# Diagonal blocks on opposite corners of the array: level 32 of the delta-rule inverse

## What is computed

```python
a_mat = jnp.where(strict, jnp.einsum('bhncd,bhnmd->bhncm', k_beta, k) * decay_mask, 0.0)
eye = jnp.eye(CHUNK, dtype=jnp.float32)
t_mat = lax.linalg.triangular_solve(a_mat + eye, jnp.broadcast_to(eye, a_mat.shape),
                                    left_side=True, lower=True)
...
def step(state, inp):
    w_c, u_c, attn_c, q_c, k_c, e_c = inp
    v_new = u_c - jnp.einsum('bhcd,bhde->bhce', w_c, state)
    o_c = jnp.einsum('bhcd,bhde->bhce', q_c, state) + jnp.einsum('bhcm,bhme->bhce', attn_c, v_new)
    state = state * e_c[..., None, None] + jnp.einsum('bhcd,bhce->bhde', k_c, v_new)
    return state, o_c
```

## Time and profile before

| | |
|---|---|
| median of 3 runs | 2157.25 us (2155.11 to 2157.98) |
| span of the profiled execution | 2150.7 us |
| TensorE busy | 2070.0 us, 96% |
| VectorE, ScalarE, GpSimd busy | 63%, 30%, 11% |
| mean granted TensorE clock | 0.993 |

### The profile page before, as it was taken

How to read it: one execution, slowest core, us unless ns; L and a number is a source line. 1 busy time by engine, 2 the same in 40 slices (tenths; PEclk the granted TensorE clock), 3 DMA queues, 4 the chain that set the end, 5 groups by cost and what they waited for, 6 DMA issues and landing times. The chain is left out here.

```text
span 2150.7 us, 20753 instructions
## 1 busy us (share of the span) xinstructions
PE 2070.0 (96%) x6898; PEld 1060.6 (49%) x6898; DVE 1364.1 (63%) x1918; ACT 642.5 (30%) x1063; POOL 234.5 (11%) x188
## 2 busy tenths in 40 slices
PE   6999999999999999999899899999999999999998
PEld 5444444446555556566555445554444444444443
DVE  4687753265746746647652578529999997534633
ACT  4345431323443434434311521012321111241021
POOL 0000001112212113122100400001000000003200
PEclk8999999999999999999999999999999999999999
DMA  9333389241111111111420316269722222334021
GB/s 342 110 109 100 116 272 236 89 92 35 47 29 37 38 37 37 24 36 43 147 41 1 108 59 120 74 189 250 173 59 75 68 73 69 103 103 137 20 98 59
DMA packets 243824, 207.17 MB, mean 96 GB/s; under 512 B 52204, under 2 KB 202785, under 8 KB 243745
## 3 DMA queue, kind: packets, MB, share of 16 engines
q1 hardware_dynamic: 213393, 157.25, 24.5%
q0 software_dynamic: 13056, 42.99, 8.2%
q10 hardware_dynamic: 17312, 6.10, 1.2%
HBM read 182.55 MB, written 60.33 MB: 113 GB/s over the span
## 5 line engine op out<-in xcount | busy, mean ns | idle before, releaser
L2300 PE MATMUL bank<-hT,ring 128*128 128x512 f32 x576 | 254.2, 592 | 0.0
L2300 PE MATMUL bank<-resid,ring 128*128 128x512 f32 x432 | 191.3, 592 | 0.0
L2300 PEld LDWEIGHTS bank<-hT,ring 128*128 128x128 f32 x576 | 109.5, 190 | 137.7 <-issue 136.7
L1279 PE MATMUL bank<-hT,ring 128*128 128x512 f32 x336 | 157.7, 595 | 1.8 <-ACT silu_z L1515 1.8
L3220 DVE SCALAR_TENSOR_TENSOR yT<-s_arena,yT 128x1024 f32<-128x1024 f32 x120 | 153.8, 1282 | 0.0
L3220 DVE SCALAR_TENSOR_TENSOR s_arena<-s_arena 128x1024 f32<-128x1024 f32 x112 | 143.5, 1282 | 0.0
L2272 PE MATMUL bank<-hT,ring 128*128 128x512 f32 x320 | 139.4, 594 | 0.0
L2300 PEld LDWEIGHTS bank<-resid,ring 128*128 128x128 f32 x432 | 82.1, 190 | 103.3 <-issue 102.3
L1869 DVE SCALAR_TENSOR_TENSOR memory<-memory,col_exp_last,bank 128x128 f32<-128x128 f32 x64 | 22.3, 348 | 153.7 <-PE bank L1459 153.7
L2272 PEld LDWEIGHTS bank<-hT,ring 128*128 128x128 f32 x320 | 60.2, 190 | 73.7 <-issue 73.4
L2345 PE MATMUL bank<-ssm_y,ring 128*128 128x512 f32 x192 | 83.4, 592 | 0.0
(11 more groups left out here) (585 smaller groups left out, 3671.7 us busy)
## 6 DMA issues: line engine op xcount, KB each, us to landing
ada<-in_ada_w SPq DMA_DIRECT2D x8, 2048.0 KB, 8.1
ring<-in_gdn_in_w SPq DMA_DIRECT2D x32, 512.0 KB, 4.1
ring<-in_w_in SPq DMA_DIRECT2D x54, 256.0 KB, 2.9
ab_U_sums<-in_w_in POOLq DMA_DIRECT2D x6, 2048.0 KB, 19.0
resid<-in_x SPq DMA_DIRECT2D x8, 1024.0 KB, 8.9
ring<-in_lru_in_w SPq DMA_DIRECT2D x16, 512.0 KB, 3.9
ring<-ab_U_sums SPq DMA_DIRECT2D x32, 256.0 KB, 3.0
lru_arena<-in_ada_w SPq DMA_DIRECT2D x6, 1024.0 KB, 12.5
```

The costliest lines, as they stand in the source:

```text
L1279: last = nc.tensor.matmul(bank[:, to, :], w[:, k, :], v[:, k, :], start=(first and k == 0), stop=(k == KB - 1), skip_group_check=not only)
L2300: last = nc.tensor.matmul(bank[:, to, :], w[:, k, :], src[:, k, :], start=(start and k == 0), stop=(k == HK - 1), skip_group_check=not alone)
```

## The change

At level 32 each chunk's 128 x 128 x 128 product becomes two 64 x 64 x 64 ones: the upper left block (`top`) and the lower right one (`under`), each on its own 64 rows and 64 columns of the array. The first matmul of each half is an exception: it reads all 128 rows, with 64 columns. This holds for `Y32` and for `YT32`, in all eight heads. Levels 16 and 64 stay as they are. And `fill(int(n == 0), 4)` becomes `fill(1, 4)`: in heads 0 to 6 one filler step now stands between `Y32` and `YT32`. In head 7 four steps stood there already.

```diff
+                    def each_half_blocks(dst, lhs, rhs, name, before):
+
+                        for n, x in enumerate("ab"):
+                            before(x)
+                            for c in range(n * NCH // 2, (n + 1) * NCH // 2):
+                                for rows_ in (top, under):
+                                    ks = slice(0, P) if (c % (NCH // 2), rows_) == (0, top) else rows_
+                                    last = nc.tensor.matmul(dst[rows_, c, rows_], lhs[ks, c, rows_], rhs[ks, c, rows_], start=True, stop=True)
+                            hd_pe.mark(last, name + x)
+
...
-                            x_, xT_ = (inv, invT) if n else (base, baseT)
-
...
-                            each_half(R4, lambda c: part[n % 2][:, c, :], lambda c: x_[:, c, :], f"Y{s}", settled)
+                            if n == 1:
+                                each_half_blocks(R4, part[1], inv, f"Y{s}", settled)
+                            else:
+                                each_half(R4, lambda c: part[0][:, c, :], lambda c: base[:, c, :], f"Y{s}", settled)
...
-                            fill(int(n == 0), 4)
-                            each_half(R4, lambda c: prod[:, c, :], lambda c: xT_[:, c, :], f"YT{s}",
-                                      lambda x: hd_act.wait(pe, f"prod{s}{x}", h))
+                            fill(1, 4)
+                            if n == 1:
+                                each_half_blocks(R4, prod, invT, f"YT{s}", lambda x: hd_act.wait(pe, f"prod{s}{x}", h))
+                            else:
+                                each_half(R4, lambda c: prod[:, c, :], lambda c: baseT[:, c, :], f"YT{s}",
+                                          lambda x: hd_act.wait(pe, f"prod{s}{x}", h))
```

## The result

The changed kernel takes 2167.28 us (median of 5 runs) against 2157.72 us before; the ratio is 1.005, 95% interval 1.0036 to 1.0065. That is slower by 7.8 to 14 us. The forecast was 2165.2 us, in a range of 2156 to 2178.5.

A forecast was written before the change was run, and what follows sets the result against it. TensorE was taken as the bound almost everywhere, VectorE at the head's end. Sixteen products at 1.93 us plus 6.02 for the filler less 28.97 removed gave +7.9 us, so 2165.2 us, range 2156 to 2178.5.

The forecast's parts named there:

- What bounds the place: Around Y32 and YT32 TensorE works without a gap; at the head's end the order of VectorE's work sets the time.
- The filler, +6.0 us: One 0.86 us step moved from the head's end to between Y32 and YT32, paid in full in seven heads.
- The work added: Each level 32 product has 32 records where it had 16, taking 1.93 us against 1.78 today.
- x: Time of one new level 32 product, first start to what follows: 1.93 us; a gain only under 1.43.
- The way in: Change of form on entering a level 32 product: 0.10 us.
- The three inner switches: Changes between 128-row and 64-row records inside a level 32 product: 0.19 us each.
- The way out: Change of form from a level 32 product to the filler behind it: 0.19 us.
- The pairing in one bank: Two blocks of a chunk write one PSUM bank on other partitions; taken to run side by side, +7.9 us, otherwise +20.9.
- No pairing: Rival: the blocks of a level 32 pair run one after the other, 2.74 us a product, 2178 us; chance 0.23.
- Cheap and free switches: Two rivals on level 32's form changes: inner ones at 0.10 us, chance 0.15; none costing anything, chance 0.12.
- Cheap ones: Rival: inner form changes at level 32 cost 0.10 us, 1.57 us a product, +2.2 us, 2159.5 us; chance 0.15.
- The sum: Whole kernel +7.9 us: +1.1 in each of seven heads and +0.3 in head 7.

The follow-up runs named there:

- one_full_row_start: Changed kernel with one 128-row matmul per product instead of one per half, both waits ahead of half a; ratio 1.0007 to the kernel before.
- double_switches: Changed kernel with four 128-row matmuls per product instead of two; ratio 1.0087 to the kernel before.
- wide_start: Changed kernel, each half's first matmul reading 64 rows and 128 columns of weights instead of 128 rows and 64 columns; ratio 1.0068 to the kernel before.
- corner_by_corner: Changed kernel with each half's four upper blocks first, then its four lower ones; ratio 1.0065 to the kernel before.
- wide_start_no_filler: Changed kernel without the added filler, each half's first matmul reading 64 rows and 128 columns of weights; ratio 1.0028 to the kernel before.

## Why the prediction was right

*What bounds the place.* Right. `Y32` and `YT32` stand without a gap, and the end of the head is set by VectorE: 8.52 us from the first left-over filler to `k_flip` in both kernels.

*The filler, +6.0 us.* Right; 5.8 us alone. `o_flip` did come 0.16 us or so sooner relative to its fillers, and it did not help, as forecast.

*The work added.* x was forecast as 1.93 us and is 1.92: 0.09 on the way in, 1.73, and 0.10 that the filler behind loses. That it fits so closely is partly luck, since the terms were off and made up for each other. The records take 20 steps, 1.17 us, for 1.07: a pair costs 0.058 as forecast, but four of the 28 records have no partner. The way in costs 0.14 (0.09 ahead of the product and 0.05 in it), for 0.10. The three inner switches cost 0.42, for 0.57: 0.14 each, for 0.19. The way out costs 0.19, as forecast.

*The pairing in one bank.* No pairing was the rival with the largest chance, and it is refuted: the records of a pair start 0.01 us apart and write to the same bank on other partitions, and both together take the 0.058 us of one. The Trainium skill (TensorEngine Tiling (Array Packing), Restrictions and Gotchas) has the rule that different row tiles cannot access the same PSUM bank at once; for these blocks, which share neither rows nor partitions, it does not set the pace. The same page of the Trainium skill says under Key Properties that a change of tiling mode drains the array; the trace agrees in that each change costs time, 0.14 us, but it does not show what the array does in it.

*Cheap and free switches.* Free ones are refuted by `one_full_row_start` and `double_switches`, whose products come out with the same 0.14 us from both sides. Cheap ones, at 0.10, are refuted too, but by less than the prediction makes it seem: 0.14 lies half way between 0.10 and its 0.19. Its price for that rival was also wrong. With only the inner switches at 0.10, x is 1.66 and not 1.57, and the time 2160.9 us; 1.57 needs the way out at 0.10 as well.

*The sum.* The forecast was 16 x 1.93 - 22.95 = +7.9 us; the head stage grew by 7.7, by 0.95 to 1.11 us in each of the seven heads (forecast 1.1) and by 0.27 in head 7 (forecast 0.3). The timed kernel lost 7.8 to 14 us in one set of runs and 5.6 to 12.3 us in the other, so 7.9 lies in both, in the first just at its edge. Single executions of the kernel before differ by up to 11 us (2151.2 to 2162.2), of which the drive's wait and clock are a part that I had not looked for.

## What to carry to other kernels

Half-size blocks on opposite corners of the array do run side by side, but each change of form costs 0.14 us, what more than two pairs of them take, and leaves records without a partner. With eight chunks in two halves, each opened by a matmul of another form, the records got 0.61 us cheaper a product (1.78 to 1.17) and the switches cost 0.75. Count the changes of form before the records, and keep whatever must differ at one end of a run, not at the start of each part. And a filler is free only where its old place was bound by TensorE: look at who sets the end of the stretch it leaves, and whether there is a gap where it goes.

## What the runs showed of the hardware that was not expected

- A change of the number of columns loaded, at the same number of rows, costs TensorE as much as a change of the rows (`wide_start` against the changed kernel, after the four wider loads).
- Records of two corners overlap even when a run of one corner's records stands ahead of the other's: 14 in 11 steps (`corner_by_corner`), where starts in the order of the queue would need 13.
- At the drive TensorE waited 2.5 to 6.2 us in ten of the thirteen profiles and had 0.50 to 0.62 of its clock in the next 4 us; in the other three it waited 0.30 to 0.88 us and had all of it. Beside the wait itself the clock cost another 1.5 to 2.9 us (the drive's first 64 records took 5.20 us in `wide_start_no_filler` and 6.63 us in the first profile of the changed kernel, for 3.71).
- The length of the wait alone does not decide it: behind the heads, after 2.2 to 2.3 us in all thirteen profiles, the same sixteen records took 7.1 us in seven and 8.7 to 8.8 us in six.
